# One bias product for eight, tiles that change place from layer to layer, a first tile in two loads, and a mix without its blocks of future keys

## The reference, cut to what matters

```python
for l in range(2):                       # first block, two layers
    h = rmsnorm(x, norm_w[l]);  proj = h @ w_in[l]
    y_a = gated_delta_branch(q_a, k_a, v_a, ab_a, z_a, ...)   # short convolution over q, k, v; 8 heads
    y_b = diff_attention_branch(q_b, k_b, v_b, z_b, cos, sin, lambda, ...)
    x = x + (sigmoid(gate_a) * (y_a @ w_pa[l]) + sigmoid(gate_b) * (y_b @ w_pb[l])) @ w_out[l]
x = rmsnorm(x, final_norm_w)
# second block, one layer
z = rmsnorm_2(x, g_mix) @ w_in_2
a_out = pool_mixer(z[..., :512])         # trailing means over 2, 4, 8, 16 tokens
b_out = dilated_attention(q, k, v, rel_bias)   # causal; 8 heads of 64; a bias per head and distance
x = x + concat([a_out, b_out]) @ w_out_2
x = x + moe(rmsnorm_2(x, g_ffn), ...)    # top 4 of 32 experts, 12 MB of weights each
x = x + (p @ w_ple_proj) * sigmoid(rmsnorm_2(x, g_ple) @ w_ple_gate);  return rmsnorm_2(x, g_final)
```

## Time and profile before

| | |
|---|---|
| median of 3 runs | 2038.42 us (2038.29 to 2040.1) |
| the profiled execution | 2040.03 us, its span 2038.3 us |
| TensorE busy | 1965.7 us, 96% |
| VectorE, ScalarE, GpSimd busy | 747.8, 425.6, 100.1 us |
| mean granted clock of TensorE | 0.996 of full |
| chain that ended last | PE 81%, DMA 16%, DVE 2%, ACT 1% |
| moved | 552.29 MB, mean 271 GB/s |

### The profile page before, as it was taken

The page is one execution under the profiler, slowest core; times in us unless marked ns, Lnnn a source line. Parts: engine busy times, 40 slices in busy tenths (PEclk is TensorE's granted clock), DMA queues, the critical chain, the costliest instruction groups (busy, mean ns, idle before and its releaser), DMA issues.

```text
span 2038.3 us, 26505 instructions
## 1 busy us (share of the span) xinstructions
PE 1965.7 (96%) x10834; PEld 1056.4 (52%) x10834; DVE 747.8 (37%) x2087; ACT 425.6 (21%) x1083; POOL 100.1 (5%) x84
## 2 busy tenths in 40 slices
PE   8999999999999999999999999999999999899997
PEld 7754567885865566885463333333333333333334
DVE  4569675212768677212143222211222122112213
ACT  2161465211042465211121000000000000000003
POOL 0021220000022121000000000000000000000000
PEclk9999999999999999999999999999999999999999
DMA  7633212343543312345859999999999999999992
GB/s 252 244 138 125 84 43 84 124 165 124 207 165 124 114 53 71 116 146 194 301 203 384 427 428 428 430 429 428 429 431 428 431 428 432 431 427 427 427 421 94
DMA packets 98820, 552.29 MB, mean 271 GB/s; under 512 B 8686, under 2 KB 13202, under 8 KB 77715
## 3 DMA queue, kind: packets, MB, share of 16 engines
q1 hardware_dynamic: 98706, 550.66, 67.1%
HBM read 547.43 MB, written 3.21 MB: 270 GB/s over the span
## 4 chain that ended last, share of the span: by engine, by line
PE 81%; DMA 16%; DVE 2%; ACT 1%; issue 1%; SPq 0%; DVEq 0%; ACTq 0%
PE bank L647 28%; DMA region<-w_gate_up_dram 15%; PE bank L1232 14%; PE bank L1264 8%; PE bank L770 6%; PE bank L1006 3%; PE bank L991 3%; PE bank L1175 2%; PE bank L1161 2%; PE bank L1090 1%; PE bank L1219 1%; DMA region<-w_in_dram 1%; PE bank L850 1%; PE bank L907 1%; PE bank L874 1%
## 5 line engine op out<-in xcount | busy, mean ns | idle before, releaser
L647 PE MATMUL bank<-region 128*128 128x256 f32 (+2 forms) x2352 | 607.6, 419 | 8.2 <-DMA region<-w_in_dram 4.4
L647 PEld LDWEIGHTS bank<-region 128*128 128x128 f32 x2352 | 442.1, 191 | 162.5 <-issue 110.3
L1232 PE MATMUL bank<-region 128*64 128x512 f32 x1872 | 415.0, 597 | 24.0 <-DMA region<-w_gate_up_dram 23.2
L1232 PEld LDWEIGHTS bank<-region 128*64 128x64 f32 x1872 | 130.8, 137 | 304.0 <-issue 262.3
L2339 DVE TENSOR_SCALAR region<-bank 128x512 f32<-128x512 f32 x32 | 22.1, 691 | 681.0 <-PE bank L1232 681.0
L1264 PE MATMUL bank<-region 128*64 128x512 f32 x944 | 209.9, 595 | 9.5 <-issue 8.0
L1264 PEld LDWEIGHTS bank<-region 128*64 128x64 f32 x944 | 77.1, 137 | 122.8 <-issue 122.8
L770 PE MATMUL bank<-region 128*128 128x512 f32 x256 | 129.2, 607 | 0.0
L1674 ACT ACTIVATE region<-region 128x512 f32<-128x512 f32 x32 | 20.2, 630 | 512.4 <-DVE region L2339 512.4
L1678 ACT ACTIVATE region<-bank 128x512 f32<-128x512 f32 x32 | 19.1, 597 | 326.8 <-PE bank L1264 326.8
L1835 DVE SCALAR_TENSOR_TENSOR region<-region,layer_mem 128x256 f32<-128x256 f32 x192 | 78.0, 477 | 0.0
(11 more groups left out here) (347 smaller groups left out, 1942.8 us busy)
## 6 DMA issues: line engine op xcount, KB each, us to landing
region<-w_gate_up_dram SPq DMA_DIRECT2D x32, 4096.0 KB, 39.0
region<-w_down_dram SPq DMA_DIRECT2D x59, 2048.0 KB, 34.3
region<-w_gate_up_dram SPq DMA_DIRECT2D x53, 2048.0 KB, 21.3
region<-w_in_dram SPq DMA_DIRECT2D x44, 2048.0 KB, 8.0
layer_mem<-w_gate_up_dram SPq DMA_DIRECT2D x11, 2048.0 KB, 35.1
region<-w_out_dram SPq DMA_DIRECT2D x6, 2048.0 KB, 8.4
layer_mem<-w_down_dram SPq DMA_DIRECT2D x5, 2048.0 KB, 36.1
region<-rows_scratch SPq DMA_DIRECT2D x4, 2048.0 KB, 9.3
```

Source lines behind the costliest of these rows:

```text
L647: mm = pe.matmul(dst, lhs(k), w(k), start=(k == 0), stop=(k == n_k - 1))
L1232: mm = pe.matmul(pb[g][hf * 64:(hf + 1) * 64, :], XT[:, 2 * (j % 2) + kk, j // 2, :], wj[:, kk, c:c + NB], start=(first and j == 0 and kk ...
```

## The change

Five things change; line numbers after it are some 5 to 11 higher.

- **Bias rows.** VectorE writes `rel_wide`, 33 by 128, in which each head's values stand in 16 neighbouring columns (after u = 5). One product of 128 columns by 512 then gives all eight heads, 16 equal rows each, after u = 7. ScalarE copies once. One transfer stores each row eight times, so `bias_scratch` holds what it held. ScalarE, no longer VectorE, waits for this store, ahead of the first exponentials of the heads.
- **Small steps earlier.** `lambda_sums` moves from u = 8 to u = 3, `angle_rows` from u = 9 to u = 4, and ScalarE's exponential and sines for them from u = 11 to u = 6.
- **Places in turns.** The count of slots runs on from layer 0 to layer 1.
- **First tile.** It comes in two loads of 1 MB, the 256 columns of u = 0 first. u = 0 waits for the first only.
- **Mix.** `CAUSAL` lists the three of the four (key tile, token tile) blocks that are not wholly in the future. The transposes, the copies, the products with v and the band products leave out the fourth.

```diff
+CAUSAL = ((0, 0), (0, 1), (1, 1))
...
-        LAYER_TILES, seen = [], [0] * SLOTS
-        for pos in range(26):
-            slot = pos % LAYER_SLOTS
-            LAYER_TILES.append((slot, seen[slot]))
-            seen[slot] += 1
-        PER_LAYER = seen
+        LAYER_LOADS = 26
+
+        def layer_tile(l, pos):
+            k, slot = divmod(l * LAYER_LOADS + pos, LAYER_SLOTS)
+            return slot, k
...
+                    if l == 0 and pos == 0:
+                        load(slot_w(slot)[:, :, 0:S], src[:, :, 0:S], "w_first")
+                        load_tile(slot_w(slot)[:, :, S:NB], src[:, :, S:NB], slot, tile_read(l, pos))
...
-                        sp.wait_ge(s("bias_rows"), H)
-                        for h0, h1 in ((0, 5), (5, H)):
-                            load(scratch[h0:h1].rearrange("h p n -> p h n"),
-                                 wk(bias_at[h0], h1 - h0).rearrange("p (h n) -> p h n", n=NB), "bias_stored")
+                        sp.wait_ge(s("bias_rows"), 1)
+                        load(scratch.rearrange("h (r i) n -> (h r) i n", i=H), bias_rows.unsqueeze(1).broadcast_to([P, H, NB]), "bias_stored")
...
-                    elif l == 0 and u in (6, 7):
-                        pe.wait_ge(s("const_in"), 16 * 9)
-                        await_once(pe, "taps_sb")
-                        for h in range(4 * (u - 6), 4 * (u - 5)):
-                            if h >= 2:
-                                pe.wait_ge(s("bias_rows"), h - 1)
-                            pe.matmul(pb[(4, 7)[h % 2]][:, :], rel[:, h:h + 1].broadcast_to([33, P]), bucket,
-                                      start=True, stop=True).then_inc(s("bias_ps"), 1)
+                    elif l == 0 and u == 7:
+                        pe.wait_ge(s("const_in"), 16 * 9)
+                        pe.wait_ge(s("rel_wide"), 1)
+                        pe.matmul(pb[4][:, :], rel_wide, bucket, start=True, stop=True).then_inc(s("bias_ps"), 1)
...
                 for m in range(2):
-                    for kt in range(NT):
-                        for t in range(NT):
-                            c = (kt * 2 + t) * P
+                    for kt, t in CAUSAL:
+                        c = (kt + t) * P
...
                 for g in range(4):
-                    mm = product(pb[2 + g // 2][:, (g % 2) * S:(g % 2 + 1) * S], lambda t: z2[:, 0, t, g * P:(g + 1) * P],
-                                 lambda t: band[:, t, g, :], NT)
+                    at = (g % 2) * S
+                    for t in range(NT):
+                        mm = pe.matmul(pb[2 + g // 2][:, at + t * P:at + S], z2[:, 0, t, g * P:(g + 1) * P], band[:, t, g, t * P:S],
+                                       start=(t == 0), stop=(t == 1), skip_group_check=True)
...
-                    if l == 0 and u in (7, 8):
-                        for h in range(4 * (u - 7), 4 * (u - 6)):
-                            act.wait_ge(s("bias_ps"), h + 1)
-                            act.activation(wk(bias_at[h]), pb[(4, 7)[h % 2]][:, :], ACT.Copy).then_inc(s("bias_rows"), 1)
-                    if l == 0 and u == 11:
+                    if l == 0 and u == 8:
+                        act.wait_ge(s("bias_ps"), 1)
+                        act.activation(bias_rows, pb[4][:, :], ACT.Copy).then_inc(s("bias_rows"), 1)
+                    if l == 0 and u == 6:
...
+                            dve.wait_ge(s("const_in"), 16 * 9)
+                            dve.tensor_copy(rel_wide.rearrange("p (h r) -> p h r", h=H),
+                                            rel[:, :].unsqueeze(2).broadcast_to([33, H, P // H])).then_inc(s("rel_wide"), 1)
...
-                    elif l == 0 and u == 8:
+                    elif l == 0 and u == 3:
                         lambda_sums()
-                    elif l == 0 and u == 9:
+                    elif l == 0 and u == 4:
                         angle_rows()
```

More of the change, by code:

```diff
@@ L318, in block_kernel @@
         gains = wk(8)[0:V_N - V_MIX, 0:P]
-        bias_at = [17, 18, 19, 20, 21, 10, 11, 12]
+        bias_rows = wk(17)
+        rel_wide = wk(18)[0:33, 0:P]
         U = units(wk(0))
@@ L389, in block_kernel @@
         block = ctx.enter_context(nc.Block())
[L392 to L397 removed]
+        LAYER_LOADS = 26
+        def layer_tile(l, pos):
+            k, slot = divmod(l * LAYER_LOADS + pos, LAYER_SLOTS)
+            return slot, k
+        IN_LAYERS = [len(range(slot, DEPTH * LAYER_LOADS, LAYER_SLOTS)) if slot < LAYER_SLOTS else 0 for slot in range(SLOTS)]
         MIX_SLOTS = (3, 4, 1, 2, 0, 5)
[L400 removed]
+        LOADED = [n + (k < 6) for k, n in enumerate(IN_LAYERS)] + [0, 0]
         AHEAD = len(TURNS)
@@ L684, in _ @@
                 for u in range(12):
-                    if u % 2 == 0:
+                    if l == 0 and u == 0:
+                        pe.wait_ge(s("w_first"), 16)
+                        w = slot_w(layer_tile(0, 0)[0])
+                    elif u < 2 or u % 2 == 0:
                         w = w_wait(l, u // 2)
@@ L1610, in pair_aT @@
                 for m in range(2):
-                    last = act.activation(aT2[:, 4 * m:4 * m + 4, :], units(pb[(7, 0)[m]][:, :]), ACT.Copy)
+                    last = act.activation(aT2[:, 3 * m:3 * m + 3, :], units(pb[(7, 0)[m]][:, 0:3 * P]), ACT.Copy)
                 last.then_inc(s("at_pT"), 1)
```

30 lines of the change are left out of this document (16 added, 14 removed).

## The result

The changed kernel takes 2028.44 us (median of 5 runs, 2025.77 to 2030.36); the kernel before took 2039.49 us on the same chip (5 runs, 2038.29 to 2040.21). The ratio is 0.9946, with a 95% interval of 0.9931 to 0.996: faster, by 11.05 us. Forecast were 2022.0 us, with a range of 2018.5 to 2028.0. The direction was right. The size was not: 16.4 us of gain were forecast, 11 came.

What follows compares the result with a forecast made beforehand. TensorE was taken to bound the first block and mix, transfers the experts; 2.4 + 8.8 + 1.6 + 3.6 = 16.4 us off the profiled 2040.03 us, less 1.6 us to the median, gave 2022.0 us, range 2018.5 to 2028.0.

Steps and rivals of the forecast that it cites:

- Start: First products: half a tile to wait for and no slow clock, capped by a late second tile; 2.4 us saved.
- Bias rows: Projections: 14 instructions fewer 6.5 us, slow stretch from 81 us gone 1.7, norm-sum wait gone 0.6; together 8.8 us.
- VectorE was no bound: Rival: VectorE becomes the bound of the projections, up to 5.9 us of the gain lost, 2027.9 us; chance 7%.
- Places in turns: Start of layer 1: the first tile lands in time and TensorE's wait goes; 1.6 us saved.
- Mix: Mix: fewer transposes 0.9 us, fewer products with v 1.8 us, narrower band products 0.9 us; 3.6 us saved.
- the rival on the other side: Rival: the clock falls in the mix, making the kernel slower, up to some 2086 us; chance 2%.
- Experts: Expert stage, paced by transfers: begins earlier by what TensorE saves before it, and keeps its length.
- The starting point: Whole run: profiled execution of 2040.03 us taken as 1.6 us above the median, 2038.42 us.
- The experts' transfers swallow the gain: Rival at the experts: their transfer stream does not begin earlier, so the end stays at 2038 us; chance 5%.
- The second slow stretch stays, or another takes its place: Rival: the low clock from 81 us stays or reappears, price 1.7 us, 2023.7 us; chance 18%.
- The rule weighed: Clock falls when TensorE idles between bursts; by it the stretch at 81 us would stay and the sum shrink.
- the stretch at 81 us: Projections: low clock directly after the second group of bias products, expected to go with one product left; 1.7 us.

Runs made afterwards that it cites:

- e6: Changed kernel with 19 small products (76 TensorE instructions) in its first idle time, and the first weight tile loaded as one transfer again: 2026.89 us.
- e11: Changed kernel with the earlier kernel's bias rows and small steps, and 12 small products in TensorE's first idle time: 2033.19 us.
- e7: Changed kernel with its bias product issued four times at u = 7, and 17 small products at the start: 2027.02 us.
- e9: Changed kernel with the bias product issued four times at u = 7 and four at u = 8, and 12 small products at the start: 2032.43 us.
- e10: Changed kernel with 19 small products (76 instructions) at the start, and each layer's weight tiles beginning at place 0 again: 2026.05 us.
- e4: Changed kernel with the mix as before (all four blocks, full bands): 2026.78 us.
- e1: Changed kernel with 19 small products (76 instructions) in TensorE's first idle time, written into a bank nobody reads: 2022.92 us.
- e2: Changed kernel with the three expert tile loads at the mix's end held until the router's last product: 2030.09 us.
- e3: The kernel before, with 45 small products (180 instructions) in TensorE's first idle time: 2049.69 us.
- e5: Changed kernel with 8 small products (32 instructions) in TensorE's first idle time: 2031.44 us.
- e8: Changed kernel with 19 small products at the start, and one small VectorE step ahead of the experts' mask issued nine times: 2026.26 us.
- e12: Changed kernel with the earlier bias rows and small steps, 12 small products at the start, and the first weight tile unsplit: 2033.76 us.

## Why the prediction was wrong

The step that failed is the one on the experts, below: that the time from the mix to the end keeps its length when instructions are removed ahead of it. It grew by 5.7 us. The other terms came out as forecast or better.

**Start: the place right, the term mis-sized.** 2.4 us were taken; 3.5 us came (23.52 to 20.05 us). e6 prices it at 4.0 us by the medians, with its wait for instructions of 0.84 us in it. The step that capped it was the second tile, "late" at 28.1 us. In the changed kernel it was issued at 15.09 us and landed 11.6 us later, at 26.7 us, ahead of its use at 27.1 us. The added load on SP's queue did not delay it.

**Bias rows: right, but for one part.** Up to the norm sums the lead grew from 3.5 to 11.74 us, and the vanished wait adds 0.63: 8.9 us, with 8.8 forecast. The parts are 6.5 us of products, 0.6 us of wait and 1.7 us of clock. e11 confirms the first two: 7.2 us with the clock full in both. The 1.7 us came too, but the reason given for them ("With one product left I expect it to go") is not borne out. Four and eight such products brought no low clock in the profiled executions of e7 and e9, nor did the old groups in e11's. As these were the fastest of their runs, the cause stays open, and that this part came may be luck. VectorE was no bound: TensorE waits for neither rel_wide nor qkv_sb.

**Places in turns: right.** 1.6 us forecast, 1.54 us in e10, and no wait at 481.61 us.

**Mix: right.** 3.6 us forecast. The lead grows from 14.3 us at layer 1 to 17.7 us behind the mix, 3.4 us; e4 gives 3.9 us by medians and 3.4 us by the traces. The clock did not fall in the mix, and the rival on the other side had no part in the result.

**Experts: the step that failed.** The prediction said: "it begins earlier by what TensorE saves before it, and its length stays". The experts' own length stayed. But between the mix's last row and the experts in the earlier trace rows lies the router, and no row of it was read. The idle DMA engines of the earlier trace rows are those of 1010 to 1020 us, in the mix. Beside the router they are full: share 0.99 in the changed kernel (1057 to 1064 us), and 0.99 in the kernel before too (1074 to 1080 us). It does not take the same time when instructions are removed ahead of it. A removed instruction was priced at its own duration, and its other effect, that it shifts where TensorE's instruction blocks end, had no term. That effect was -5.7 us of +17.7: 1.9 us of waiting for a late block and 3.8 us of half clock behind it. The experiments close in on it from several sides: the same loads with another count (e1), no wait; the same count without loads (e2), no wait; the old kernel with the new alignment (e3), the wait; another shift (e5), the wait at the shifted place.

**The starting point: 1.1 us.** The prediction took 1.6 us off the profiled execution's time, because that lay 1.6 us above the median of three runs. Above the median of all five, 2039.49 us, it lies 0.5 us. From that median the same sum of 16.4 us gives 2023.1 us, not 2022.0. So of the 6.4 us between forecast and result 1.1 us are the starting point's. The profiled spans differ by 12.0 us: the 16.4 us forecast and 1.3 us more ahead of the router (1.1 of it at the start), less the 5.7 us lost. The medians differ by 0.9 us less than that, which is within their scatter.

**The rivals.** "The experts' transfers swallow the gain" named the right stretch of the run for a wrong reason. "The second slow stretch stays, or another takes its place" was the nearest: it was priced at 1.7 us, for one fall of 4 us, and its likely place was sought where products are narrow. The fall came where TensorE had to wait, lasted nearly three times as long and cost 3.8 us besides the wait.

**The rule weighed.** That the clock falls when TensorE stands idle between bursts was held against the stretch at 81 us, and the sum went against it. The experiments speak for the rule more than the prediction did: 1.31 us of added idleness bring the fall in the router (e8), and each of the waits for instructions there (1.52, 1.77 and 4.86 us) has one behind it. But a wait by itself does not decide it: 1.43, 1.59 and 1.60 us elsewhere brought none. Ahead of the stretch at 81 us no idleness is shown, and it stays unexplained.

On the fetch itself, the Trainium skill (Runtime: NRT & Kernel Launch, Instruction fetch mechanics) says that the sequencer fetches blocks of 16 KiB by its own DMA queue and that crossing a boundary costs a step that is "mostly hidden". The size agrees with the 85 packets of 1.39 MB. Mostly hidden agrees too, since in the changed kernel TensorE has no other wait for "issue" of more than 0.4 us; but the one that was not hidden took, with the clock behind it, a third of the lead.

Open are: what the unprofiled runs of e7, e9 and e11 lost against their profiled ones (2 to 3.7 us), the clock at 81 us, why one wait brings half clock and another as long does not, and why the half clock lasts 3.4 us in one case and 10 in another.

## What to carry to other kernels

When a change removes or adds instructions ahead of a stage that floods the DMA queues, look behind it for a wait whose releaser is "issue", with a packet on the instruction queue beside it; if there is one, pad or trim the instruction count in idle time before judging the change. An edit's whole worth, here the mix's 3.9 us, can hang on that alignment, so parts should be priced at a like alignment. And a forecast that adds up removed work should name every stretch between the edits and the end, also those in which nothing changes.

## What the runs showed of the hardware

- TensorE stood idle for "issue" for 0.84 us (e6), 1.52 us (e3), 1.60 us (e12), 1.77 us (the changed kernel), 4.86 us (e5) and 5.09 us (e3), in each case while weight tiles were being loaded. With the DMA engines idle (share 0.02) the same block cost nothing and its packet moved 3.2 us earlier against the program (e2). A packet that met full DMA engines at another place cost nothing either (e1).
- In all six of these waits an instruction packet moved during the wait or up to 2 us before it, and TensorE went on 2.3 to 2.9 us after the packet (1060.4 and 1062.84 us in the changed kernel, 1061.9 and 1064.24 in e5, 497.2 and 499.86 in e3).
- 76 instructions more at the start made the kernel 5.5 us faster (2022.92 against 2028.44 us). With 32 more its median was 3.0 us higher (2031.44 us), with ranges that overlap.
- 1.31 us more without work brought half clock in the router, for one group of 3.53 us in place of 1.94 (e8). 1.59 us at layer 1 of the kernel before and 1.60 us in e12 brought none. 1.02 us at the start has a slow product behind it in e10 and none in e1 (8.75 and 7.14 us).
- Loads started 10.4 us later, ahead of a stage bound by transfers, added 5.9 us to its waits (27.8 against 21.9 us), more than the wait that this cured.
